# Replicating the sample queries across partitions: ScalarE copies in place of a TensorE product, in a one-core decoder step

## The reference, cut to what matters

```python
gate = jnp.einsum('bhqd,bhnd->bhqn', qb.astype(jnp.float32), kmean)
logits = jnp.einsum('bhqd,bhqskd->bhqsk', qb, k_sel).astype(jnp.float32) * scale + bias.astype(jnp.float32)
...
kv = rmsnorm(mem, norm_w) @ w_kv
```

## Time and profile before

| | us |
|---|---|
| median of 3 runs | 650.11 |
| lowest, highest | 649.38, 651.97 |
| profiled execution, its own time | 650.07 |
| its span, first to last instruction | 648.4 |
| TensorE busy | 629.1 (97%) |
| VectorE busy | 405.7 (63%) |
| ScalarE busy | 152.3 (23%) |
| GpSimd busy | 139.0 (21%) |

### The profile page before, as it was taken

One profiled execution on the slowest core, in us unless ns is written; L12 is line 12 of the kernel. 1 busy time (PEld: TensorE's weight loads), 2 busy tenths in 40 slices (PEclk: granted clock), 3 DMA queues, 4 the chain that ended last, 5 costly groups with the idle time before them and its releaser, 6 DMA issues.

```text
span 648.4 us, 13116 instructions
## 1 busy us (share of the span) xinstructions
PE 629.1 (97%) x4877; PEld 504.6 (78%) x4877; DVE 405.7 (63%) x879; ACT 152.3 (23%) x409; POOL 139.0 (21%) x222
## 2 busy tenths in 40 slices
PE   8999999999999999999999999999999999999995
PEld 6766776676676655557667876899999999999995
DVE  3466576997764667777423346887887874553733
ACT  3110020001212875783102333211211110000001
POOL 6152212110220026151001100433443540000000
PEclk9999999999999999999999999999999999999998
DMA  8798998897942158878696551344544535534501
GB/s 311 242 295 258 290 295 262 243 289 243 286 134 66 66 194 249 311 184 248 199 324 233 210 194 66 112 149 131 171 155 138 187 132 183 176 131 150 172 5 74
DMA packets 98779, 125.75 MB, mean 194 GB/s; under 512 B 6571, under 2 KB 74687, under 8 KB 98722
## 3 DMA queue, kind: packets, MB, share of 16 engines
q1 hardware_dynamic: 92818, 106.62, 50.9%
q0 software_dynamic: 5648, 18.14, 8.9%
q10 hardware_dynamic: 256, 0.20, 0.1%
HBM read 116.64 MB, written 8.31 MB: 193 GB/s over the span
## 4 chain that ended last, share of the span: by engine, by line
PE 77%; DVE 3%; ACT 1%; issue 1%; DVEq 0%; ACTq 0%
PE ps L1618 34%; PE ps L1194 25%; PE ps L1151 4%; PE ps L1261 3%; PE ps L1427 1%; PE ps L1214 1%; PE ps L1373 1%; PE ps L1309 1%; PE ps L1157 1%; PE ps L1303 1%; PE ps L1285 1%; PE ps L1417 1%; PE ps L1406 1%; PE ps L1236 1%; PE ps L1292 1%
## 5 line engine op out<-in xcount | busy, mean ns | idle before, releaser
L1194 PE MATMUL ps<-hw,wring 128*128 128x288 f32 x576 | 148.4, 413 | 0.4 <-DVE big L2126 0.4
L1194 PEld LDWEIGHTS ps<-hw,wring 128*128 128x128 f32 x576 | 108.1, 192 | 37.3 <-issue 6.9
L2253 DVE STREAM_TRANSPOSE tmp<-big 128x1024 f32<-128x1024 f32 x32 | 37.9, 1222 | 2.5 <-PE ps L1214 2.4
L1005 POOL TENSOR_TENSOR acc<-acc,sq 128x288 f32<-128x288 f32 (+1 forms) x35 | 29.3, 836 | 31.5 <-ACT sq L1842 29.3
L2099 DVE COPY tmp<-ps 128x512 f32<-128x512 f32 (+6 forms) x35 | 21.5, 619 | 21.3 <-PE ps L1151 16.0
L1618 PE MATMUL ps<-hw,wring 128*128 128x144 f32 x256 | 34.2, 287 | 0.0
L1618 PE MATMUL ps<-big,wring 128*128 128x144 f32 x256 | 34.0, 286 | 0.0
L1618 PEld LDWEIGHTS ps<-hw,wring 128*128 128x128 f32 x256 | 32.5, 190 | 0.4 <-DVE hw L2103 0.4
L1194 PE MATMUL ps<-big,wring 128*128 128x288 f32 x128 | 32.7, 409 | 0.0
L1194 PE MATMUL ps<-attT,wring 128*128 128x288 f32 x128 | 31.9, 407 | 0.7 <-DVE hT L2148 0.7
L1618 PEld LDWEIGHTS ps<-big,wring 128*128 128x128 f32 x256 | 32.4, 190 | 0.0
(11 more groups left out here) (352 smaller groups left out, 1150.9 us busy)
## 6 DMA issues: line engine op xcount, KB each, us to landing
wring<-in_w_in SPq DMA_DIRECT2D x16, 1024.0 KB, 7.1
wring<-in_w_up SPq DMA_DIRECT2D x16, 1024.0 KB, 5.1
wring<-in_w_down SPq DMA_DIRECT2D x16, 1024.0 KB, 4.7
big<-in_cache_v SPq DMA_DIRECT2D x56, 256.0 KB, 3.5
big<-in_cache_k SPq DMA_DIRECT2D x36, 256.0 KB, 3.5
big<-in_cache_k POOLq DMA_DIRECT2D x28, 256.0 KB, 4.2
wring<-in_w_out SPq DMA_DIRECT2D x6, 1024.0 KB, 5.8
wring<-in_w_ca_kv SPq DMA_DIRECT2D x4, 1024.0 KB, 8.2
```

Of the source, the lines that this page charges most:

```text
L1005: pool.tensor_tensor(a, a, sq[:, m % 2, 0:n], ALU.add).then_inc(acc_done, 1)
L1194: last = pe.matmul(ps[:, BANK[key], 0:width], w, rhs, start=(k == 0), stop=(k == K_TILES[kind] - 1))
L2253: dve.transpose(KT_[:, step_ % 2].rearrange("p c (w j) -> p w c j", j=32), src[:, :, :, m, :])\
```

## The change

The item `qrep` no longer has a product. ScalarE copies each group of 32 partitions of the sample queries, 32 x 256, to each of the four groups, in 16 copies, when tile qk(1,1) is done. GpSimd's weight copies wait for the last of these (`qrep_made`). The two bank turns and evictions go. In `SEQ` the item `qrep` stands ahead of `memt 3`, so the copies are ahead of ScalarE's last two memory squares. GpSimd's additions are split: six stay where they were, the last two come at `memt 3`, behind its weight copies and page loads. The item `ss mem` moves from inside the first key unit to behind it, directly ahead of `tab`.

```diff
@@ make_plan
     item("memt", 2)
+    item("qrep")
     item("memt", 3)
-    item("qrep")
-    keys(0, 0, "qk", 2, ("ss", "mem"))
+    keys(0, 0, "qk", 2)
+    item("ss", "mem")
     item("tab")
@@ plan_turns
         elif s[0] == "qrep":
-            turn(("qrep", 0)), turn(("qrep", 1))
+            continue
@@ GpSimd
-            def add_squares(name, n):
+            def add_squares(name, n, lo=0, hi=DT):
                 k = NORM[name]
-                for c in range(DT):
+                for c in range(lo, hi):
...
-                    turned(pool, ("qrep", 0)), turned(pool, ("qrep", 1))
+                    pool.wait_ge(qrep_made, 1)
...
                 if s == ("memt", 0):
-                    add_squares("mem", NP_)
+                    add_squares("mem", NP_, 0, 6)
+                elif s == ("memt", 3):
+                    add_squares("mem", NP_, 6, DT)
@@ TensorE
-                elif s[0] == "qrep":
-                    tile_done(pe, ("qk", 1, 1))
-                    for m in range(4):
-                        key = ("qrep", m // 2)
-                        if m % 2 == 0:
-                            bank_free(pe, key)
-                        for a in range(4):
-                            last = pe.matmul(ps[32 * a:32 * a + 32, bank(key), m % 2 * 256:m % 2 * 256 + 256],
-                                             ident[:, 32 * m:32 * m + 32], qsf[:, 0:256], start=True, stop=True,
-                                             tile_position=(0, 32 * a))
-                        if m % 2:
-                            last.then_inc(turn_ps, 1)
@@ ScalarE
                 elif s[0] == "qrep":
-                    leave(("qrep", 0)), leave(("qrep", 1))
+                    tile_done(act, ("qk", 1, 1))
+                    for m in range(4):
+                        for a in range(4):
+                            last = act.activation(qrep[32 * a:32 * a + 32, 4 * m:4 * m + 4].rearrange("p k b e -> p (k b e)"),
+                                                  qsf[32 * m:32 * m + 32, 0:256], ACT.Copy)
+                    last.then_inc(qrep_made, 1)
```

More of the change, by code:

```diff
@@ L709, in build @@
         sq_done, acc_done, rstd_done = sem("sq_done"), sem("acc_done"), sem("rstd_done")
+        qrep_made = sem("qrep_made")
         hw_done, memw_done, zeros_made, qs_clear = sem("hw_done"), sem("memw_done"), sem("zeros_made"), sem("qs_clear")
@@ L1715, in turn_targets @@
                 return vv[:, :], ps[:, b, 0:T]
-            if kind == "qrep":
-                i = key[1]
-                return qrep[:, 8 * i:8 * i + 8, :, :].rearrange("p k b e -> p (k b e)"), ps[:, b, :]
             if kind in ("ktok", "mktok"):
```

## The result

The changed kernel takes 661.88 us (median of 6 runs, 657.82 to 663.51); the kernel before, run beside it, takes 649.75 (6 runs, 648.75 to 651.97). The ratio is 1.0175, with an interval of 1.0147 to 1.0203: 1.75% slower, 12.1 us where 4.05 were forecast, and outside the range of 652.6 to 657.0.

What follows compares the result with a forecast made beforehand. TensorE, busy 629.1 of 648.4 us, was taken as the bound. Earlier key products -0.25, late additions +0.8 and the open chain +3.5 gave +4.05 us on 650.07, so 654.1 us; range 652.6 to 657.0.

Steps and rivals of the forecast that it cites:

- qk(2,0) starts right behind the transposes: TensorE, after the memory input's transposes: with the product gone the tile begins at 33.50 instead of 36.86, freeing 3.36 us.
- the two places named: TensorE waits of about 3.5 us ahead of the first key products and about 3 us ahead of the bias tables.
- The open chain: Moved row sum, root, reciprocal, table operands: no other TensorE work covers them before the bias tables; +3.5 us.
- Nothing behind swallows a delay: TensorE behind the bias tables: full from there on, so the +4.05 us stays; only 1.35 us idle between 100 and 111.
- a granted clock of 1.00 throughout: TensorE across both new waits: the clock stays at full rate, so no slow matmuls were priced in.
- the fall as a rival at 0.15: TensorE's clock halves in the new wait, key products and part of the tile slow, 1.4 to 3.5 us more: 656; chance 0.15.
- at its edge or below: Argument against a clock fall: new waits of 3.5 and 3.0 us against some 3.4 us idle before the tail's fall.
- The rule of the Trainium skill that the prediction weighed: TensorE: leave no longer idle gaps between matmul bursts, or the clock returns to half rate; by it, 656 us.
- The term of the copies: ScalarE's 16 copies, 0.31 us apart and 0.42 for the last: 5.1 us, ending at 40.3.
- -0.25: First key products: TensorE begins them at about 41.1 instead of 41.37, a gain of about 0.25 us.
- the rival of copies without overlap: ScalarE's copies take 0.442 us each, end at 42.3 and shift all behind by 1.8 us: 655.9; chance 0.05.
- The 0.8 us for the additions: Ahead of the moved row sum: GpSimd's last two additions, behind weight copies and page loads, keep TensorE waiting 0.8 us.

Runs made afterwards that it cites:

- a3: The kernel before, product and evictions kept, with only the row sum moved behind the first key unit, directly ahead of the bias tables: 656.11 us, ratio 1.0092.
- a1: The changed kernel with unread products in TensorE's two waits, 22 ahead of the first key products and 12 ahead of the bias tables: 655.61 us, ratio 1.0103.
- a2: The kernel before with its product replaced by the 16 ScalarE copies, in the old order of items, additions unsplit: 654.63 us, ratio 1.0081.
- a5: The changed kernel, each copy reading the group of 32 partitions that it writes (queries not the reference's): 664.66 us, one run.
- a8: The changed kernel with the two copy loops exchanged, so the written group stays for four copies while the read one changes: 663.73 us, one run.
- b1: The kernel before with its product replaced by 16 copies on VectorE, in the old order of items: 654.87 us, ratio 1.0054.
- a7: The changed kernel with copy loops exchanged and each copy reading the group it writes (queries not the reference's): 657.42 us, one run.
- after_again: The changed kernel, unaltered, run again for a second profile: 661.7 us, ratio 1.0185 to the kernel before.
- a6: The changed kernel with 22 unread products in TensorE's first wait alone: 658.33 us, ratio 1.0141.
- a4: The changed kernel with four copies of 128 partitions instead of 16 of 32 (queries not the reference's): 656.59 us, ratio 1.0114.
- c1: The kernel before, product kept, its two results sent to banks 4 and 5 to avoid waiting for ScalarE's square: 650.24 us, ratio 0.9992.

## Why the prediction was wrong

**What held.** qk(2,0) starts right behind the transposes (aligned 33.33 for 33.5). TensorE then waits twice, at the two places named. The open chain is worth 3.63 us (3.5 forecast), in a3 3.20 against before, in a1 3.58. Nothing behind swallows a delay: the spacing to before's starts stays at 7.3 us from 63 to 280 us (11.6 when aligned). The direction and its reason, an order in which no work covers the chain, were right, but they are only a third of the loss.

**What failed: that the clock holds.** The prediction said "a granted clock of 1.00 throughout", with the fall as a rival at 0.15. It fell in both waits, and cost 2.43 + 4.19 = 6.6 of the 12 us in the first trace, 2.58 + 1.41 = 4.0 of 11.05 in the second. a1 removes both falls; the end comes 5.4 us earlier than in the first trace, with the additions' 1.19 us now in the open. Two judgements were wrong. I called 3.5 and 3.0 us of idle time "at its edge or below", from one row at the tail, where the fall came after some 3.4 us; a3 fell 2.3 us after the last matmul, and over all waits of this stretch the fall came 2.0 to 4.3 us after it. One row at one place was read as a limit. And I priced the rival at 1.4 to 3.5 us, for one fall, with TensorE back at full speed within the tile; the second fall here lasted through the tables and the memory tile, 9 us of busy time. The rule of the Trainium skill that the prediction weighed (TensorE: Matmul & The Clock Gate, "Why this matters for your kernels") is borne out in kind, and its rival came closest, though even that was 6 us short.

How much a fall costs is no constant. The fall in the first wait cost 2.43 and 2.58 us in the two traces of the changed kernel, 1.72 in a2, 2.21 in a5, 2.28 in a8, 2.11 in b1 and 1.42 in a7. That in the second wait, 2.93 us each time, cost 4.19, 4.21 (a3), 4.08 (a5) and 4.12 (a8) in one set of executions, 1.41 (after_again), 1.37 (a6) and 1.58 (a4) in the other, and nothing in a7. The same program gave 4.19 and 1.41, so the program alone does not decide it. The granted clock, read in windows of 0.5 us, shows what goes with it. In the four dear cases the clock had fallen 0.64 to 0.90 us before TensorE came back (at 50.73 for 51.41 in the first trace), and it stayed at 0.50 for 10.2 us. In after_again and a4 it fell 0.51 and 0.18 us before the return, in a6 0.40 us behind it, and it stayed at 0.50 for 3.4 us. In the first wait it is alike: 6.8 us at 0.50 in all but a7, where the fall came 0.12 us behind TensorE's return and 3.4 us were slow. Why the clock falls earlier or later in the same wait stays open.

**The term of the copies was mis-sized.** 0.31 us each, from 48 scaled copies in a row; measured 0.42, since each copy changes its group of partitions and so does not overlap the one ahead (a5, a7, a8). The rows I used were all of one group. That makes the copies 1.7 us longer, and "-0.25" became +1.33. This is close to the rival of copies without overlap (0.442 us each, 7.1 in all), given 0.05; I argued against it from rows that differ in just the property that mattered. It also made the first wait 5.3 us instead of 3.5.

**The 0.8 us for the additions** is 0 in the changed kernel, because TensorE itself arrives late, and 1.19 where the clock is kept (a1). The reasoning was sound, the cover came from a loss elsewhere.

**What to make of the sum.** Forecast: -0.25 + 0.8 + 3.5 = 4.05. Shown: 1.33 + 0 + 3.63, plus 6.62 for the clock, plus 0.43 late: 12.0. Without the falls of the clock the kernel is at a1's 655.6 us, 1.5 above my forecast. The range would have held that, but partly by luck: the first term would still be 1.6 us too low.

**Open.** Why the clock falls at different points of the same wait, and so costs 4.2 us or 1.4; why the clock falls near 250 us in about half of the traces (a4, a5, a7, a8, after_again, c1), in kernels with and without the change, while TensorE is full; why one execution of fourteen had TensorE at full speed in its first stage. No kernel here that does the replication beats the one before by more than can be told.

## What to carry to other kernels

On an engine that is busy 97% of the time, a wait has two prices: its length, and the slower clock of the work behind it. Here 8.3 us of waits (5.32 and 2.93) cost 4.0 to 6.6 us more in slow matmuls; so a change that trades busy time of TensorE for waits like these should be priced with a fall of the clock at each of them, and work moved into the gap (as in a1) checks it cheaply. A row sum must stay far ahead of its user when a root and a reciprocal lie between: moving it next to the user opened 3.6 us that key products and a tile had covered. And copies of a few partitions should be ordered so that the groups read and written stay the same, or be priced one after the other without overlap.

## What the runs showed of the hardware that I had not expected

- ScalarE overlaps two 32 x 256 copies (0.31 us apart) only if both read and write the groups of partitions of the one ahead; else they are 0.42 us apart (16 copies: 5.34 against 6.78 us).
- In seven of the eight traces with the wait of 2.93 us the clock fell: in six within the wait, 2.0 to 2.8 us after the last matmul, in a6 3.3 us after it, 0.4 us behind the wait. Where it fell, the work behind lost 1.4 to 4.2 us: 4.1 to 4.2 with 10.2 us at 0.50, 1.4 to 1.6 with 3.4 us.
- The granted clock also fell to 0.50 with TensorE busy 2.00 of 2.00 us (244 to 246 us in c1), for a loss of 1.7 us.
- In the first stage the granted clock can read 1.00 while the matmuls run at half speed: the same 24 transposes took 6.95 us in the kernel before and 4.41 in the first trace of the changed one, both at 1.00.
